# Two of the four weight combinations of a crossed MLP unit move from VectorE to accumulating transfers

## What is computed

```python
x = x + merged @ w_out[layer]
h2 = rms_norm(x, g_mlp[layer])
x = x + jnp.square(jax.nn.relu(h2 @ w_mlp_in[layer])) @ w_mlp_out[layer]
return rms_norm(x, g_final)
```

## Time and profile before

| | |
|---|---|
| median of three runs | 1622.26 us (1622.06 to 1622.46) |
| span of the profiled execution | 1620.0 us |
| TensorE clock, mean granted | 0.999 |
| ScalarE busy | 917.1 us |
| VectorE busy | 1264.1 us |
| GpSimd busy | 79.1 us |
| read from HBM | 308.68 MB |

### The profile page before, as it was taken

The page is one execution under the profiler, slowest core; times in us unless marked ns, Lnnn a source line. Parts: engine busy times, 40 slices in busy tenths (PEclk is TensorE's granted clock), DMA queues, the critical chain, the costliest instruction groups (busy, mean ns, idle before and its releaser), DMA issues.

```text
span 1620.0 us, 20751 instructions
## 1 busy us (share of the span) xinstructions
PE 1608.5 (99%) x8104; PEld 1362.2 (84%) x8104; DVE 1264.1 (78%) x1520; ACT 917.1 (57%) x1262; POOL 79.1 (5%) x67
## 2 busy tenths in 40 slices
PE   9999999999999999999999999999999999999998
PEld 7888888888888888888888888888888888888886
DVE  7888878888666677776665576999799988998893
ACT  6666556666565445544444555665556556655562
POOL 3000000000001134000000000000000000000000
PEclk9999999999999999999999999999999999999999
DMA  7666665666556664445576676458646764586471
GB/s 272 202 200 190 189 200 189 208 195 203 183 186 182 191 187 153 142 145 175 187 229 195 225 236 187 144 182 285 184 125 224 262 190 134 194 282 209 148 245 53
DMA packets 134194, 312.21 MB, mean 193 GB/s; under 512 B 9744, under 2 KB 10448, under 8 KB 133968
## 3 DMA queue, kind: packets, MB, share of 16 engines
q1 hardware_dynamic: 129376, 302.21, 58.4%
q10 hardware_dynamic: 4720, 8.68, 2.0%
HBM read 308.68 MB, written 2.16 MB: 192 GB/s over the span
## 4 chain that ended last, share of the span: by engine, by line
PE 96%; DVE 2%; issue 1%; ACT 0%; POOL 0%; DMA 0%; POOLq 0%; DVEq 0%
PE G L1719 17%; PE G L1720 17%; PE G L1721 17%; PE G L1728 13%; PE S L1728 7%; PE G L1732 6%; PE S L1719 4%; PE S L1721 4%; PE S L1720 4%; PE S L1732 4%; PE S L1740 1%; PE S L1847 1%; DVE wlo L1022 1%; PE S L1891 0%; PE S L1824 0%
## 5 line engine op out<-in xcount | busy, mean ns | idle before, releaser
L637 ACT ACTIVATE whi<-raw 128x1024 fp32r<-128x1024 f32 x395 | 417.0, 1059 | 418.1 <-PE G L1721 254.9
L1022 DVE TENSOR_TENSOR wlo<-raw,whi 128x1024 fp32r<-128x1024 f32 x395 | 482.5, 1236 | 128.7 <-ACT whi L637 127.4
L1719 PE MATMUL G<-whi,a_both 128*128 128x512 f32 x768 | 301.3, 392 | 2.3 <-DVE wlo L1022 1.7
L1721 PE MATMUL G<-whi,a_both 128*128 128x512 f32 x768 | 299.5, 390 | 0.0
L1720 PE MATMUL G<-wlo,a_both 128*128 128x512 f32 x768 | 299.5, 390 | 0.0
L1728 PE MATMUL G<-a_both,whi 128*128 128x512 f32 x640 | 201.7, 397 | 0.0
L1719 PEld LDWEIGHTS G<-whi,a_both 128*128 128x128 f32 x768 | 144.3, 188 | 33.3 <-issue 2.6
L1721 PEld LDWEIGHTS G<-whi,a_both 128*128 128x128 f32 x768 | 144.2, 188 | 30.1
L1720 PEld LDWEIGHTS G<-wlo,a_both 128*128 128x128 f32 x768 | 144.3, 188 | 28.7
L1732 PEld LDWEIGHTS G<-a_both,wlo 128*128 128x128 f32 x640 | 120.3, 188 | 28.2
L1719 PE MATMUL G<-whi,b_hi 128*128 128x512 f32 x342 | 133.9, 392 | 0.0
(11 more groups left out here) (306 smaller groups left out, 2692.4 us busy)
## 6 DMA issues: line engine op xcount, KB each, us to landing
raw<-in_w_in SPq DMA_DIRECT2D x208, 512.0 KB, 4.3
raw<-in_w_mlp_in SPq DMA_DIRECT2D x74, 512.0 KB, 4.0
raw<-in_w_mlp_out SPq DMA_DIRECT2D x74, 512.0 KB, 5.0
gates<-in_w_mlp_in SPq DMA_DIRECT2D x54, 512.0 KB, 4.0
gates<-in_w_mlp_out SPq DMA_DIRECT2D x54, 512.0 KB, 4.9
raw<-in_w_ssm_up SPq DMA_DIRECT2D x32, 512.0 KB, 3.8
raw<-in_w_attn_up SPq DMA_DIRECT2D x32, 512.0 KB, 4.6
raw<-in_w_out SPq DMA_DIRECT2D x32, 512.0 KB, 4.6
```

Source lines behind the costliest of these rows:

```text
L637: act.activation(high(m), piece(n), ACT.Copy).then_inc(hi_made, 1)
L1022: dve.tensor_tensor(low(m), piece(n), high(m).bitcast(F32), ALU.subtract).then_inc(lo_made, 1)
L1719: pe.matmul(out_ap, hi[:, k, cols], w_hi, start=start, stop=False)
L1721: return pe.matmul(out_ap, lo[:, k, cols], w_hi, start=False, stop=stop)
```

## The change

Before, four combinations of a crossed unit are VectorE subtractions. After, two are VectorE additions (t1 = b11 + b12, right after the low part of b11; t4 = b21 + t2, after the low part of t2), and two are DMAs with addition into the destination, issued by GpSimd: b12 += b22 gives t3, b22 += t1 gives t2. To make all four additions, signs are turned in the sums of the hidden values and in the mixing of the products. Each combination has a semaphore of its own. The second DMA waits for the first. Raw slots are released later for two of the four pieces. The identity matrix moves to the end of SBUF, and the space for descriptors is 1024 in place of 512.

```diff
+SUM_STEP = {"t1": 1, "t3": 16, "t2": 16, "t4": 1}
-SUM_TURN = {"t1": 1, "t3": 2, "t2": 3, "t4": 4}
...
-    return BLOCK[n] + (4, 5, 6, 7)[part]
+    return BLOCK[n] + (6, 5, 7, 7)[part]
...
-                act.wait_ge(t_made, turn + SUM_TURN[block])
+                act.wait_ge(sum_made[block], SUM_STEP[block] * (crossed_before(g, q, unit) + 1))
             high_part(m, n)
...
-            if i == 0:
-                low_part(m, n)
-            if i == 1:
-                dve.wait_ge(landed[piece_slot(n + 1)], landings(n + 1))
-                dve.wait_ge(lo_made, m)
-                difference(n, n + 1, n)
-                low_part(m, n + 2)
-            if i == 2:
-                difference(n + 1, n + 2, n + 1)
-                low_part(m, n)
-                dve.wait_ge(lo_made, m)
-                difference(n + 2, n + 2, n)
-            if i == 3:
-                low_part(m, n + 3)
-                dve.wait_ge(t_made, turn + 3)
-                dve.wait_ge(lo_made, m + 1)
-                difference(n + 3, n + 3, n + 2)
-            if i > 3:
-                low_part(m, n + i - 3)
+            block = PAIR_BLOCKS[i]
+            low_part(m, n + (PAIR_FROM[block] if block in PAIR_FROM else SUM_INTO[block]))
+            if block == "b11":
+                dve.wait_ge(landed[piece_slot(n + 1)], landings(n + 1))
+                dve.wait_ge(lo_made, m + 1)
+                dve.tensor_tensor(piece(n), piece(n), piece(n + 1), ALU.add).then_inc(sum_made["t1"], 1)
+            if block == "t2":
+                dve.wait_ge(lo_made, m - 1)
+                dve.tensor_tensor(piece(n + 3), piece(n + 3), piece(n + 2), ALU.add).then_inc(sum_made["t4"], 1)
...
-                dve.tensor_tensor(s_sum[:, 0, :, :], a21, a22, ALU.add).then_inc(s_v, 1)
-                dve.tensor_tensor(s_sum[:, 2, :, :], a11, a21, ALU.subtract).then_inc(s_v, 1)
+                dve.tensor_tensor(s_sum[:, 0, :, :], a21, a22, ALU.subtract).then_inc(s_v, 1)
+                dve.tensor_tensor(s_sum[:, 2, :, :], a21, a11, ALU.subtract).then_inc(s_v, 1)
...
+        def add_blocks(n):
+
+            g, q, unit, _ = pair_place(n)
+            turn, m = 16 * (crossed_before(g, q, unit) + 1), BLOCK[n]
+            b11, b12, b22 = (piece(n + part) for part in range(3))
+            pool.wait_ge(sum_made["t1"], turn // 16)
+            pool.wait_ge(landed[piece_slot(n + 2)], landings(n + 2))
+            pool.dma_start(b12, b22, accum_op=ALU.add).then_inc(sum_made["t3"], 16)
+            pool.wait_ge(lo_made, m + 2)
+            pool.wait_ge(sum_made["t3"], turn)
+            pool.dma_start(b22, b11, accum_op=ALU.add).then_inc(sum_made["t2"], 16)
...
+                n = piece_number(r, par, p)
+                if crossed(n) and pair_place(n)[3] == 0:
+                    add_blocks(n)
...
-    nc = bacc.Bacc("TRN2", target_bir_lowering=False, num_devices=1, dynamic_dma_scratch_size=512)
+    nc = bacc.Bacc("TRN2", target_bir_lowering=False, num_devices=1, dynamic_dma_scratch_size=1024)
```

More of the change, by code:

```diff
@@ L276, in align @@
         top[0] = -(-top[0] // n) * n
-    ident = place("ident", [P, P])
+    usable_end = nc.sbuf_usable_end // 64 * 64 - 4 * P
+    ident = nc.alloc_sbuf_tensor_at("ident", [P, P], F32, offset=usable_end)
     gains = place("gains", [P, 3 * KT])
@@ L379, in build @@
     wdt = place("wdt", [P, TB, HEADS])
-    assert top[0] <= nc.sbuf_usable_end, (top[0], nc.sbuf_usable_end)
+    assert top[0] <= usable_end, (top[0], usable_end)
     top[0] = region_r
@@ L469, in build @@
     row_mm = sem("row_mm")
-    t_made, s_v, s_hi_made, s_lo_made = sem("t_made"), sem("s_v"), sem("s_hi_made"), sem("s_lo_made")
+    sum_made = {block: sem(f"sum_{block}_made") for block in SUM_INTO}
+    s_v, s_hi_made, s_lo_made = sem("s_v"), sem("s_hi_made"), sem("s_lo_made")
     h_taken, c_taken = sem("h_taken"), sem("c_taken")
@@ L645, in split @@
             g, q, unit, _ = pair_place(n)
-            turn = 4 * crossed_before(g, q, unit)
             block = PAIR_BLOCKS[i]
@@ L1022, in low_part @@
             dve.tensor_tensor(low(m), piece(n), high(m).bitcast(F32), ALU.subtract).then_inc(lo_made, 1)
-        def difference(n, of, less):
-            dve.tensor_tensor(piece(n), piece(of), piece(less), ALU.subtract).then_inc(t_made, 1)
         def split(m):
@@ L1484, in hidden @@
                 turn = 4 * (len(SUMMED) * g + j)
-                dve.tensor_tensor(s_sum[:, 0, :, :], a21, a22, ALU.add).then_inc(s_v, 1)
-                dve.tensor_tensor(s_sum[:, 2, :, :], a11, a21, ALU.subtract).then_inc(s_v, 1)
+                dve.tensor_tensor(s_sum[:, 0, :, :], a21, a22, ALU.subtract).then_inc(s_v, 1)
+                dve.tensor_tensor(s_sum[:, 2, :, :], a21, a11, ALU.subtract).then_inc(s_v, 1)
                 dve.wait_ge(s_v, turn + 1)
-                dve.tensor_tensor(s_sum[:, 1, :, :], s_sum[:, 0, :, :], a11, ALU.subtract).then_inc(s_v, 1)
+                dve.tensor_tensor(s_sum[:, 1, :, :], a11, s_sum[:, 0, :, :], ALU.subtract).then_inc(s_v, 1)
                 dve.wait_ge(s_v, turn + 3)
@@ L1514, in mixed @@
                 dve.wait_ge(m_out, 2 * turn + 2)
-                dve.tensor_tensor(m[:, 1, :], m[:, 0, :], m[:, 1, :], ALU.add).then_inc(mix_v, 1)
+                dve.tensor_tensor(m[:, 1, :], m[:, 0, :], m[:, 1, :], ALU.subtract).then_inc(mix_v, 1)
                 dve.wait_ge(mix_v, 4 * turn + 1)
-                dve.tensor_tensor(m[:, 2, :], m[:, 1, :], m[:, 2, :], ALU.add).then_inc(mix_v, 1)
+                dve.tensor_tensor(m[:, 2, :], m[:, 1, :], m[:, 2, :], ALU.subtract).then_inc(mix_v, 1)
             if p == 6:
@@ L1525, in mixed @@
                 dve.wait_ge(mix_v, 4 * turn + 3)
-                dve.tensor_tensor(m[:, 1:3, :], m[:, 1:3, :], m[:, 3, :].unsqueeze(1).to_broadcast([P, 2, N]), ALU.add
+                dve.tensor_tensor(m[:, 1:3, :], m[:, 1:3, :], m[:, 3, :].unsqueeze(1).to_broadcast([P, 2, N]), ALU.subtract
                                   ).then_inc(mix_v, 1)
@@ L1529, in mixed @@
                 dve.wait_ge(mix_v, 4 * turn + 4)
-                dve.tensor_tensor(own[:, 1, :, :], own[:, 1, :, :], m[:, 1:3, :], ALU.add).then_inc(x_mixed, 1)
+                dve.tensor_tensor(own[:, 1, :, :], own[:, 1, :, :], m[:, 1:3, :], ALU.subtract).then_inc(x_mixed, 1)
         def mix_out(p, idx, pr, pp):
@@ L1535, in mix_out @@
                 dve.wait_ge(mix_a, 1)
[L1536 to L1540, removed]
+                dve.tensor_tensor(mt[:, 1, 1, :], mt[:, 0, 0, :], mix_bank(q, 1), ALU.subtract).then_inc(mix_v, 1)
+                dve.wait_ge(mix_v, 25)
+                dve.tensor_tensor(mt[:, 0, 1, :], mt[:, 1, 1, :], mix_bank(q, 2), ALU.subtract).then_inc(mix_v, 1)
+                dve.tensor_tensor(mt[:, 1, 0, :], mix_bank(q, 3), mt[:, 1, 1, :], ALU.subtract).then_inc(mix_v, 1)
+                dve.wait_ge(mix_v, 27)
+                dve.tensor_tensor(mt[:, 1, 1, :], mix_bank(q, 3), mt[:, 0, 1, :], ALU.subtract).then_inc(mix_v, 1)
                 dve.wait_ge(mix_v, 28)
```

2 lines of the change are left out of this document (removed).

## The result

| | before | changed |
|---|---|---|
| median of the runs, us | 1622.16 (1621.90 to 1622.46) | 1701.01 (1699.54 to 1706.66) |
| profiled execution, us | not given apart | 1706.66 |
| its span, us | 1620.0 | 1704.5 |

The changed kernel takes 1.0492 times as long (95% interval 1.0479 to 1.0505), 78.9 us more; the forecast was 1703. The profiled execution lies 5.7 us above the median of its own runs.

The account below looks back on a forecast made before the run. TensorE, busy 1608.5 of 1620.0 us, was taken as the bound. Removed VectorE work counted 0; two serial transfers at L = 6.0 us made 80.6 us of lateness, giving 1703 us, range 1630 to 1820.

Parts of the forecast that it names:

- The bound and the removed work: TensorE bounds the kernel; removing 34 VectorE additions, 41.5 us busy, in crossed units is worth 0 on the path.
- The chain of one unit: In a crossed unit, two transfers in series, splits and an addition make t4 ready 2L + 5.8 us after t1.
- The price L: Time of one accumulating 512 KB transfer on GpSimd's queue: taken as 6.0 us, between 3.2 and 10.0.
- The sum: Lateness over the groups: three times 25.3 us and 4.7 for g = 3, 80.6 us in all, giving 1703 us.
- The prediction's own working: Unit-by-unit reckoning of t4's readiness from 2L against TensorE's wanted start; lateness stays, 80.6 us at L = 6.0.
- The slope of 34: Once the chain over crossed units is unbroken, each us of L costs 34 us.
- Signs, identity, descriptor space: Turned signs, the identity's moved place and the larger descriptor space were each put at 0 us.
- Slot releases: Raw slots held longer were put at nothing: the next unit's b21 load has 1.9 us of cover.
- Not slower: Rival: transfers below 2.8 us, freed VectorE time widens the lead, 1622 us; chance 0.10.
- barely slower: Rival: L from 2.8 to 3.5, TensorE late in the third unit alone, up to 1636 us; chance 0.05.
- GpSimd held by VectorE: Rival: each transfer's issue is held for one VectorE operation, 1.22 us more, L = 7.2, 1744 us; chance 0.13.
- The DMA engines as the bound: Rival: transfers queue behind load bursts in the crossed stretch, L 9 or more, 1839 us at L = 10; chance 0.12.

Follow-up runs that it names:

- e8: Changed kernel with both transfers of a unit as plain copies, the additions into t3 and t2 left out: 1661.1 us, 1.0243 of before.
- e10: Changed kernel with both transfers cut to half of the columns, 256 KB each, the other half not formed: 1665.1 us, 1.0267 of before.
- e11: Changed kernel with each transfer as two of 256 KB, the second's first half waiting only for the first's first half: 1685.3 us, 1.0386 of before.
- e6: Changed kernel with a small GpSimd operation, and a wait for it, ahead of each of the 34 transfers: 1708.4 us, 1.0532 of before.
- e9: e5 with the raw slots released as in the kernel before: 1622.1 us, 0.9999 of before.
- e5: Changed kernel with all four additions on VectorE and t4's addition back behind b21's low part: 1627.4 us, 1.0032 of before.
- e4: Changed kernel with all four additions on VectorE, plus 30 transfers of 512 KB into a buffer at rest: 1635.6 us, 1.0081 of before.
- e7: Changed kernel with five zero-weight matmuls ahead of TensorE's waits for t2 and t4, except in each column pair's first unit: 1693.3 us, 1.0440 of before.

## Why the prediction was right, step by step

**The bound and the removed work.** Right: two additions a unit less on VectorE gave nothing back, and TensorE was kept waiting only inside crossed units. Nearly all waits of the list are for low parts, and 1130 to 1200 us runs full at clock 1.00.

**The chain of one unit.** Right: t4 was to be ready 2L + 5.8 behind t1. In the unit shown, the second transfer was issued at 1041.7 and landed 4.4 later, at 1046.1, which makes 2L = 10.2 and t4 due at 1051.9; TensorE started it at 1052.0. The third unit of pair 1 was forecast to be 25.3 us late and was 24.7.

**The price L.** Mis-sized: 6.0 forecast, 5.6 measured in the mean, where the landings and the time before each issue are both in it. The bottom-up sum of the prediction mixed them: it made 6.3 us out of a load and 512 KB more, but the undisturbed transfer is 4.4 us. What lifts it is the queue (0.3 and 0.6 us) and, for the first transfer, mainly the loads beside it (median 5.4, up to 7.6 us). The estimate of 4.4 us for 1 MB from the Trainium skill (DMA: Bandwidth & Descriptors, Anatomy of one DMA; Collectives: The Full Stack, The bandwidth ceiling) is the undisturbed landing of this trace. But it isn't what the chain paid, and the 1658 us that followed from it were 43 too low. That an addition is paid as a second read agrees with e8 and e10.

**The sum.** That 1703 and 1701 lie so close is in part luck. The prediction's own working, with the mean chain of each kernel's profiled execution put in for 2L, against the medians:

| | 2L, mean us | the working gives | measured over before |
|---|---|---|---|
| e8 | 7.98 | 25 | 39 |
| e10 | 8.38 | 30 | 43 |
| e11 | 9.92 | 50 | 63 |
| changed kernel | 11.24 | 68 | 79 |
| e6 | 11.64 | 75 | 86 |

The working gives the differences between the kernels within 3 us; this is the strongest evidence for the mechanism. But it is 11 to 14 us short in each, and the forecast was met because an L that was too high, worth 13 us (81 against 68), stood against this. The slope of 34 holds only for L above 5.6. Below it the slots and not the chain set the second unit, and the same working has about 26 for each us. That is why e8, forecast with 34, took longer than expected with shorter landings.

The trace shows what the shortfall is made of, for its 84.5 us. With each unit's own chain, as measured, in place of the mean, the working gives 71 us: the transfers of column pair 1, which count, take longer than the others. Steps of a few tenths that it leaves out (the first t1 of pair 1 comes 9.8 us after t4 was ready, not 9.1) make 4 more, which gives the 75.0 at the last t4 of the groups; 80.6 were forecast there. The clock behind them adds 9.3. For the median of the runs the shares aren't known.

**What was carried at nothing.** Signs, identity, descriptor space: right (e9, 0.9999). Slot releases: I had given them 1.9 us of cover at the next unit's b21 and stopped there. With VectorE making all additions they cost 5.3 us, by a plain piece and, behind it on ScalarE, the eviction mix_out (e5). Beside the transfers no such cost is seen: TensorE's list has no wait for an eviction, and ScalarE's waits for loads from 990 us on add up to 6.9 us, against 38 in e5. The longest groups of these, in the changed kernel and in e5:

```profile
ACT whi_late L639 <- DMA raw<-in_w_mlp_out: 4.2, 6, 1.0
...
ACT whi_late L639 <- DMA gates<-in_w_mlp_out: 10.0, 5, 3.6
```

So nothing shows that the 5.3 us are part of the sum; the changed kernel with the old releases wasn't run. The clock: not mentioned at all, although the waits that I forecast were just what it falls behind.

**The rivals.** Not slower or barely slower would have needed L up to 3.5; even a plain copy has 4.0 in the chain (7.98 / 2), because the queue's 0.3 and 0.6 us and the loads beside the first transfer come on top of its 2.8. GpSimd held by VectorE: no. The issues of the changed kernel take 0.86 us, although VectorE runs without a gap during 15 of the 17 first ones, and the longest of all 34 takes 1.06, so none was held for an operation of 1.22 us:

```profile
L1692 POOL DMA_DIRECT2D raw<-raw x7: 859/872/1057, 1015.7 to 1622.9; - x7
```

The DMA engines as the bound: no. Nearly the same traffic beside the work costs a few us at most (e4), and the plain loads land as before. The loads lengthen only the first transfer, by 1.0 us in the median. No version here beats the kernel before, whose TensorE is busy 99% of the span. What wasn't tried is to start a unit's transfers a unit earlier: it would need more raw slots.

## What to carry to other kernels

Where an engine with lead is relieved, the saving is nothing, and the question is only the latency of what replaces it: put its landing, counted from the start of the issue, and the queue's turn-round before it into one step price, count the steps in series, and compare with the pitch of the bound engine. Two steps of 5.6 us in place of two additions, 2.3 us, took a chain past the 9.5 us pitch of its unit, and from there each unit passed its lateness on. Changes that look like bookkeeping (when a buffer is released) need the same walk through every queue that waits for the buffer, and each forecast wait of TensorE needs a term for the clock behind it.

## What the runs showed of the chip that I had not expected

- One packet of an accumulating transfer of 512 KB kept its DMA engine busy for 294 ns, of a plain copy of the same size for 142 (changed kernel, e8).
- An accumulating transfer of 512 KB, SBUF to SBUF, 128 rows of 4 KB: 4.4 us from issue to landing with the engines free, 256 KB 3.2 us, a plain copy of 512 KB 2.8 us. Issuing takes 0.86 us with addition and 0.53 without, and doesn't depend on the row's length (e10); from a landing to the next issue that waited for it pass 0.6 us, from a VectorE operation to it 0.3.
- An issue right behind another is on record for 1.21 us instead of 0.86, but overlaps it by 0.32, so two in a row take 1.75 us (e11).
- Beside bursts of plain loads the same transfer took up to 7.6 us. In the changed kernel two of them fall between 1060 and 1075 us, the first of them among loads (packets, MB and share of the engines for GpSimd's queue, then for the loads' queue):

```profile
q0 software_dynamic: 288, 1.05, 35.3%
q1 hardware_dynamic: 1048, 2.01, 34.7%
```

GpSimd's 1.05 MB took as much of the engines' time as 2.01 MB of loads. Two landings of 6.8 and 6.2 us (issued at 1015.7 and 1216.9) had next to no loads beside them, but each a transfer of the `instruction` queue; whether that was the cause wasn't tested.
- Waits of up to 3.8 us in an otherwise full stream of matmuls brought stretches at 1.2 GHz, 64.9 us in all, of which 9.3 us of time weren't covered by later waits in the execution seen. With matmuls put into the waits, most of them were gone, and the time fell by 7.7 us (e7).
